# A hybrid attention step on one core: the load queue's head, two runs of small transposes and the first level of the gated scores in another form

## The reference

```
m = silu(cond) @ w_ada + b_ada                # 6 x 1024 values for each of the two conditions
h = rmsnorm(x, g_mix) * (1 + sc1) + sh1       # sh1, sc1: the first two sixths of m
u = h @ w_in                                  # columns: gated q, k, v, r | zf, zb (2 x 16) | attention q, k, v | gates
la = log_sigmoid(z @ w_alpha + b) / 16        # decay of each token and channel, from zf and zb
# gated part, per head, within a tile of tokens:
scores[t, s] = sum_d q[t, d] k[s, d] exp(b[t, d] - b[s, d]),  s <= t   (and its mirror for the other direction)
# attention part:
o = softmax([q k_near^T * scale + bias, q cache_k^T * scale]) @ [v_near, cache_v]
x = x + gt1 * mix(gated, attention);  x = x + gt2 * conv_ffn(h2)
```

## Time and profile before

| | |
|---|---|
| time of three runs (median, lowest, highest) | 969.75, 969.64, 969.89 us |
| the profiled execution: its own time, its span | 970.44, 968.6 us |
| PE busy, of the span | 952.3 us, 98% |
| DVE, ACT, POOL busy | 603.2, 434.7, 503.9 us |
| moved by DMA | 108.20 MB, mean 112 GB/s |
| the granted clock of PE | full in all 40 slices |

### The profile page before, as it was taken

The page is one execution under the profiler, slowest core; times in us unless marked ns, Lnnn a source line. Parts: engine busy times, 40 slices in busy tenths (PEclk is TensorE's granted clock), DMA queues, the critical chain, the costliest instruction groups (busy, mean ns, idle before and its releaser), DMA issues.

```text
span 968.6 us, 18808 instructions
## 1 busy us (share of the span) xinstructions
PE 952.3 (98%) x7513; PEld 866.9 (89%) x7513; DVE 603.2 (62%) x1087; ACT 434.7 (45%) x683; POOL 503.9 (52%) x361
## 2 busy tenths in 40 slices
PE   6999999999999999999999999999999999999998
PEld 5799899977888899999987999999999999888886
DVE  6508359963575769434937998777777778903002
ACT  5244165523766564342404465555555556511110
POOL 1386723323332317772724378888888885433331
PEclk9999999999999999999999999999999999999999
DMA  9896222126011133888641313222222222322331
GB/s 335 270 157 97 78 76 55 58 77 185 23 30 38 45 86 100 265 251 296 236 152 44 88 45 87 88 86 84 82 83 82 83 83 72 121 81 82 105 107 55
DMA packets 127826, 108.20 MB, mean 112 GB/s; under 512 B 8342, under 2 KB 104571, under 8 KB 127483
## 3 DMA queue, kind: packets, MB, share of 16 engines
q1 hardware_dynamic: 122728, 99.81, 34.1%
q0 software_dynamic: 1696, 3.25, 2.3%
q10 hardware_dynamic: 3315, 3.94, 1.1%
HBM read 101.45 MB, written 4.47 MB: 109 GB/s over the span
## 4 chain that ended last, share of the span: by engine, by line
PE 87%; DVE 5%; SPq 2%; issue 2%; POOL 1%; ACT 1%; DMA 1%; DVEq 0%; POOLq 0%; ACTq 0%
PE PA L1649 6%; PE PA L1647 6%; PE PA L1648 6%; PE PJ L923 6%; PE PJ L928 5%; PE PJ L924 5%; PE PA L1533 3%; PE PA L1535 3%; PE PA L1534 3%; PE PJ L1533 3%; PE PJ L1535 3%; PE PJ L1534 3%; PE PJ L1441 2%; PE PA L1367 2%; PE PJ L1442 2%
## 5 line engine op out<-in xcount | busy, mean ns | idle before, releaser
L713 POOL TENSOR_TENSOR wlo<-wraw,whi 128x1024 fp32r<-128x1024 f32 x53 | 133.1, 2513 | 257.4 <-ACT whi L1704 167.4
L923 PE MATMUL PJ<-h_hi,whi 128*128 128x320 f32 x336 | 104.8, 320 | 0.1
L924 PE MATMUL PJ<-h_lo,whi 128*128 128x320 f32 x336 | 101.1, 309 | 0.0
L928 PE MATMUL PJ<-h_hi,wlo 128*128 128x320 f32 x336 | 76.5, 309 | 0.0
L1704 ACT ACTIVATE whi<-wraw 128x1024 fp32r<-128x1024 f32 x39 | 41.0, 1052 | 71.8 <-PE PJ L928 23.2
L923 PEld LDWEIGHTS PJ<-h_hi,whi 128*128 128x128 f32 x336 | 63.0, 188 | 5.8 <-issue 3.6
L2220 ACT ACTIVATE whi<-wraw 128x1024 fp32r<-128x1024 f32 x21 | 22.3, 1060 | 98.6 <-PE PA L1535 51.6
L924 PEld LDWEIGHTS PJ<-h_lo,whi 128*128 128x128 f32 x336 | 63.1, 188 | 0.0
L880 POOL TENSOR_TENSOR behind<-behind_val,behind 128x512 fp32r<-128x512 f32 x40 | 52.0, 1301 | 19.0 <-ACT behind L2199 19.0
L1649 PE MATMUL PA<-h_hi,behind 128*128 128x320 f32 x192 | 59.3, 309 | 0.0
L928 PEld LDWEIGHTS PJ<-h_hi,wlo 128*128 128x128 f32 x336 | 56.1, 188 | 0.0
(11 more groups left out here) (593 smaller groups left out, 3234.3 us busy)
## 6 DMA issues: line engine op xcount, KB each, us to landing
wraw<-in_w_in_dram SPq DMA_DIRECT2D x72, 256.0 KB, 3.2
ada_rest<-in_w_ada_dram SPq DMA_DIRECT2D x32, 512.0 KB, 6.1
wraw<-in_w_up_dram SPq DMA_DIRECT2D x48, 256.0 KB, 3.8
wraw<-in_w_down_dram SPq DMA_DIRECT2D x42, 256.0 KB, 3.0
raw_even<-in_w_up_dram SPq DMA_DIRECT2D x40, 256.0 KB, 3.6
ada<-in_w_ada_dram SPq DMA_DIRECT2D x16, 512.0 KB, 7.5
out_dram<-x ACTq DMA_DIRECT2D x10, 256.0 KB, 2.1
x_rows<-in_x_sample_dram SPq DMA_DIRECT2D x2, 1024.0 KB, 6.5
```

The lines of the kernel that those rows point to most:

```text
L713: pool.tensor_tensor(wlo[:, slot, 0:k, :], wraw[:, slot, 0:k, :], whi[:, slot, 0:k, :].bitcast(F32), ALU.subtract).then_inc(lo_done, done)
L923: pe.matmul(out, whi[:, slot, w0 + k, :], hi(k)[:, tok], start=start and k == k0, stop=False)
L924: pe.matmul(out, whi[:, slot, w0 + k, :], lo(k)[:, tok], start=False, stop=False)
L928: mm = pe.matmul(out, wlo[:, slot, w0 + k, :], hi(k)[:, tok], start=False, stop=stop and k == k1 - 1)
```

## The change

Six edits, all at the head of the kernel or in the gated part:

1. In SP's program `w_z` and the half `ada_half(1, 1)` are issued ahead of the chunk of the second tile of columns, `w_z` first.
2. Four transposes of the identity are put at the very start of PE's program, after the wait for the identity. They write columns of PSUM that nothing else writes before level 0.
3. In the loop over groups `low_rank(g)` stands ahead of `modulation_rows(g + 1, 1)`.
4. The cached keys are transposed by `by_rows`: 16 products of 64 rows in place of 8 of 128.
5. ACT's copy of them reads the two banks through `from_halves`.
6. Level 0 takes products of 64 by 64, as the other levels do, but only of the blocks on the diagonal: 40 matmuls in place of 20. The blocks off the diagonal aren't written; the mask of level 0 doesn't take them.

```diff
@@ block.sync
             ada_half(1, 0)
-            chunk(0, 0, w_in_v, P, None)
-            ada_half(1, 1)
             sp.wait_ge(tab_in, 16)
             sp.dma_start(w_z[:, :, :], w_in_v[:, :, IN_Z:IN_Z + 32]).then_inc(tab_in, 16)
+            ada_half(1, 1)
+            chunk(0, 0, w_in_v, P, None)
@@ block.tensor
             pe.wait_ge(tab_in, 16)
+            for at_ in (1344, 1408, 1856, 1920):
+                unread(1, at_)
             pe.wait_ge(cvec_in, 16 * 3)
...
                     modulation_rows(1, 0)
+                low_rank(g)
                 if g < ADA_GROUPS - 1:
                     modulation_rows(g + 1, 1)
-                low_rank(g)
                 if g < ADA_GROUPS - 1:
                     rows_to_columns(g + 1)
...
-                    tr = pe.transpose(PA[:, j * PAST + b * P:j * PAST + (b + 1) * P], kc_tok[:, b, j * P:(j + 1) * P], ident[:, :])
+                    tr = by_rows(lambda i: psum("PA", i), (2 * j + b) * 64, kc_tok[:, b, j * P:(j + 1) * P])
...
-                            for h in range(2 if n else 1):
+                            for h in range(2):
                                 for r in range(2):
-                                    at_, m = 64 * h, 64 if n else P
+                                    at_, m = 64 * h, 64
@@ block.scalar
-                    act.activation(kcT[:, :, :].rearrange("p a b -> p (a b)"), PA[:, 0:1024], ACT.Copy).then_inc(kct_cp, 1)
+                    act.activation(kcT[:, :, :].rearrange("p j (b i n) -> p (j b) i n", i=2, n=64), from_halves(PA[:, 0:1024]), ACT.Copy)\
+                   .then_inc(kct_cp, 1)
```

## The result

The changed kernel takes 972.84 us (median of 17 runs, 971.30 to 974.14); the kernel before, run beside it on the same chip, 970.32 us (17 runs, 969.57 to 972.33). The ratio is 1.0023, interval 1.0016 to 1.0030: 0.16 to 0.30% slower, 2.5 us between the medians. The forecast was +1.49 us. The profiled execution of the changed kernel took 974.05 us and its span is 972.3 us, against 970.44 and 968.6 before.

What follows compares the result with a forecast made beforehand. PE was taken to bound the kernel, busy 952.3 of 968.6 us. Terms: +1.51 (group 0) + 1.32 (groups 1 and 2) - 0.30 (keys) - 1.04 (level 0) = +1.49 us on 969.75, so 971.2 us; range 969.3 to 973.0.

Steps and rivals of the forecast that it cites:

- prediction's own mark of 971.7 us: Whole kernel: above this time it counts as slower, about 0.2% (1.94 us) being what a measurement can tell; chance 0.38.
- Rival two: Load queue, group 0: z's thin stretch comes ahead of the chunk, which lands near 27.6 us; 972.4 us, chance 0.2.
- Rival three: PE in group 0: its clock falls to the lower level after some 2.4 us standing still; +1.3 us, chance 0.08.
- The chunk and the copy behind `wlo`: Group 0: late chunk delays DVE's subtraction, the copy of group 1's rows behind it, and PE's turning; 1.77 us lost.
- Given back at group 2: PE ahead of group 2's first half: it now comes after the weights have landed, so 0.26 us of waiting goes.
- Groups 1 and 2: Turnings there: z's products go first and no longer cover DVE's copy; cost 2 x 0.66 = 1.32 us.
- Cached keys: Key transposes on PE: 16 loads of half rows replace eight of 128x128; 0.3 us gained, ends 0.1 and 0.37.
- Level 0: Level 0 to the projection behind it: 2.43 us becomes level 1's 1.39; 1.04 us gained, ends 0.9 and 1.1.
- Early transposes: Start of PE's program: four transposes run while PE has nothing to do; worth nothing, up to 0.1 us either way.
- Rival four: Load queue, group 0: load order doesn't decide the landing, chunk there by 24.6 us, no cost; 969.7 us, chance 0.14.
- five: Head: chunk lands by 24.6 us and DVE's copy costs PE less; 968.7 us, 967.9 with 0.87 us saved, chance 0.06.
- no instruction of PE back at its longer duration after 29 us: Sign in the changed kernel's trace: PE's instructions do not go back to the slower pace after group 0.

Runs made afterwards that it cites:

- experiment three: Changed kernel plus 20 unread transposes of the identity where PE stood still in group 0; 972.22 us, ratio 1.0014 to the kernel before.
- Experiments four: Changed kernel with z's products first in group 0 only, groups 1 and 2 in the old order; 972.11 us, ratio 1.0020 to the kernel before.
- six: Kernel before with z's products ahead of the modulation half in groups 1 and 2 only; 971.99 us, ratio 1.0010.
- Experiments one: Changed kernel with the old load order and z's products in their old place; 969.62 us, ratio 0.9994 to the kernel before.
- experiment eight: Kernel before with level 0, keys and early transposes changed, plus a DVE wait for POOL's fifth down-projection subtraction; 969.25 us, ratio 0.9979.
- experiments two: Kernel before with only the new load order and z's products first in every group; 973.81 us, ratio 1.0041.
- seven: Kernel before with the new load order alone; 972.61 us, ratio 1.0019.
- nine: Kernel before plus only a DVE wait for POOL's fifth down-projection subtraction; 970.22 us, ratio 0.9997.
- experiment ten: Changed kernel plus a DVE wait for POOL's fifth down-projection subtraction; 972.72 us, ratio 1.0023 to the kernel before.
- five: Changed kernel with the old load order, z's products still first everywhere; 971.19 us, ratio 1.0004 to the kernel before.

## Why the prediction came out as it did

The time lies in the range, by 0.16 us, and above the 972.3 that was the end of the forecast's own range. By the prediction's own mark of 971.7 us the change is slower, to which it gave 0.38 against 0.58 for the same. The range held because rivals two and three had pushed its end to 973.0; and 0.57 us of the 972.84 is that the kernel before ran at 970.32 in place of 969.75. By steps:

- **The chunk and the copy behind `wlo`** (1.77 us): right in mechanism, 1.52 us in size. ACT began at 26.33 us for 26.4, `wlo` was through at 28.65 for 28.72, the turning came at 28.90 for 29.15. Of the 0.25 us, 0.07 is the landing, 0.12 the copy's start, which the rows show 0.09 us ahead of the end of `wlo`, and 0.06 the step from copy to turning, 0.34 us for 0.40.
- **Given back at group 2** (0.26 us): right. The idle time went; from the first product to group 2's half it took 2.25 us, and 1.93 in experiment three at clock 1.00: 0.32 us.
- **Groups 1 and 2** (2 x 0.66 us): oversized. It was 0.49 and 0.48 us, 0.97 in all; the table's first step of 0.57 holds 0.09 us of the low clock. Before, the half's start to the turning took 34.40 - 32.85 = 1.55 us with z's products in it; now z's products take 0.57 us ahead of the half and 1.47 us follow from its start, of which 0.41 idle: 2.04 us, 0.49 more. I had taken z's 0.66 us as the whole price and set nothing against it, though the products read 0.09 us shorter ahead of the half. The rest is that the half and the copy behind it need 1.47 us, where I reckoned 1.55. Experiments four and six show the size again.
- **Cached keys** (0.30 us gained, 0.1 to 0.37): 0.04, below the range. PE needs 0.65 us to the next projection in place of 0.79, and 0.39 us from the products ahead in place of 0.29: the changeovers, which I had taken as equal, are longer. Experiments one and eight show 1.03 and 1.04 us from those products to the projection, two, six, seven and nine, with the old keys, 1.08 or 1.09.
- **Level 0** (1.04 us): 1.03. **Early transposes** (nothing): no row shows PE later or earlier by them; no run isolates them.
- **Rival two**, which I gave 0.2: its thin stretch did come ahead of the chunk, but the chunk was no later for it. The small packets (under 512 bytes), which are z's, stood at 24 to 25 us before and at 19 to 21 us now, as the last section shows; the same bytes were through at 26.37 us before and 26.33 now. Rival four fell with the chunk's landing at 26.33, and five with it.
- **Rival three**, which I gave 0.08, is what happened. Priced at +1.3 us, it cost 1.50. The sentence of the prediction that failed is "no instruction of PE back at its longer duration after 29 us". I argued from 0.87 us of idle time, after which the products ran at their old pace, to 2.4 us. That a row shows a short gap harmless says nothing of one three times as long, and the profile's only other evidence, 421 ns at the start, pointed the other way. Even that is no clean evidence: the granted clock of those windows (6 to 9 us) reads 1.00, before and after, and in the changed kernel it reads 1.00 through the 2.82 us of idle time behind the early transposes as well. At the start the reading and the pace of PE don't agree, and no run settles it. The Trainium skill, page "TensorE: Matmul & The Clock Gate", Part 1, which says that an idle PE goes to 1.2 GHz and which the prediction set aside as shown by no row, is borne out by the 0.50 of the changed kernel's window.

Of the 17 runs of the changed kernel, three lie at 971.30 to 971.39 us, at clock 1.00: near the forecast's 971.2, and partly by luck, since without the clock's 1.50 the sum is +1.1 us on 970.32, where the forecast was +1.49 on 969.75. One more at 1.00 took 972.34, what the stall would make of them. Of the other 13, 11 are at 0.998 or 0.997 and two at 0.999, which may be either; seven lie from 972.31 to 973.04 and six from 973.66 to 974.14. The profiled execution of 974.05, with fall and stall, is of the last kind. For that one kind the sum is seen: +1.52 - 0.32 + 1.50 + 0.97 - 0.04 - 1.03 = +2.6 us, as the table's row behind level 0 has it, and 0.9 for the stall: +3.5; measured +3.61 on the execution's own time. In the others I infer the stall from their times; only profiled runs show it, and experiment ten has a run of 974.27 with the wait against it in place. That the median's excess (2.5 us) and the sum without the stall (2.6) agree is partly luck, since some runs have no fall and some, by their times, the stall.

The stall is open in part. It appears in five of the nine profiles without the wait of experiment eight (the changed kernel, experiments one, three, six and seven). One, six and seven have no edit in common, and two, four and five, with much the same edits, don't have it. Its two instructions start 0.4 us apart, and which one holds the other up changes with no edit near them. So I take it for chance and no term of the change, with unlike shares in the medians. But the one profile of the kernel before is free of it, and experiment nine's gain of 0.4 us in the median is within the noise: that the kernel before has it too, or that the change makes it more frequent, the runs can't say. Nor is it settled why some executions of the changed kernel keep the clock through a gap of the same kind.

## What to carry to other kernels

Ask of a wait that is taken away which instruction stands in front of the answer on the third engine. Here a load moved later by 3.2 us held up the products that need it, and its rounding sat in DVE's stream ahead of a copy that PE needed too. No run put the copy ahead of the subtraction. By the rows PE could then have turned at about 26.8 us (an estimate: rows ready at 26.4, 0.4 us for the copy), and have stood for some 1.6 us until `wlo` was done; whether the clock survives that is open. Price a gap that opens on PE twice: its length, and the same work behind it at the lower clock; where PE had to wait for 2.5 us, unread work in the gap delayed nothing and kept the clock. And take the local gains (quadrants, half rows) by themselves before they are sold together with a new order.

## What the runs showed of the hardware

- The fall of the clock: in the stretch from 22 us on, 1.00 through idle times of 0.87 us, and of 1.03 and 0.41 us; 0.50 for some 3.4 us after 2.3 to 2.6 us of idleness in every profile that had such a gap unfilled (the changed kernel, experiments two, four, seven and ten); 1.00 when 20 transposes, whose output nobody reads, stood in it.
- POOL's and DVE's tensor_tensor instructions hold one another up: POOL's 2.4 us became 6.37 beside five of DVE's back to back, while in other executions with the same start it took 2.71 and the five took 5.97. With a wait that fixes the turn none of three profiles has the stall (eight, nine and ten); without it five of nine have.
- The rate of the load queue is low where z's small packets are (its load is 1024 runs of 128 bytes), and the low place moves with them. One microsecond of each kernel, 24 to 25 us before and 19 to 20 us after (20 to 21 us after: 393 small ones and 340 GB/s):

```profile
DMA packets 958, 0.26 MB, mean 260 GB/s; under 512 B 801, under 2 KB 958, under 8 KB 958
```

```profile
DMA packets 818, 0.30 MB, mean 301 GB/s; under 512 B 597, under 2 KB 818, under 8 KB 818
```

  The thin stretch behind it, 287 GB/s at 26 to 28 us before, is something else: 26 of its 570 packets are small. The six profiles with the old load order have 243 to 323 GB/s there, the six with the new one 368 to 379; why is open.
